# A three-stack transformer kernel whose first norm is applied after its first two products, and whose modulation slabs are spread later over the opening

## What is computed

```python
h = rmsnorm(x, norm_mix)                      # x * rsqrt(mean(x*x) + eps) * gain
proj = h @ w_in                               # qa, ka, va, ra, a_lr, qb, kb, vb, gates
log_a = log_sigmoid(a_lr @ w_lr_up + b_forget) / TAU
...
mod_lat = silu(c) @ ada_w[i] + ada_b[i]       # modulation rows, needed only by the second stack
```

## Time and profile before

| | us |
|---|---|
| median of 3 runs | 1387.56 (1385.98 to 1390.21) |
| the profiled execution | 1386.29, of which its span 1384.5 |
| PE busy in the span | 1356.4 |
| opening: m2's first product / m24's first product | 28.81 / 212.01 |
| longest wait of PE | 7.6, at the start |

### The profile page before, as it was taken

One profiled execution on the slowest core, in us unless ns is written; L12 is line 12 of the kernel. 1 busy time (PEld: TensorE's weight loads), 2 busy tenths in 40 slices (PEclk: granted clock), 3 DMA queues, 4 the chain that ended last, 5 costly groups with the idle time before them and its releaser, 6 DMA issues.

```text
span 1384.5 us, 25206 instructions
## 1 busy us (share of the span) xinstructions
PE 1356.4 (98%) x10086; PEld 1236.2 (89%) x10086; DVE 1017.7 (74%) x1330; ACT 856.9 (62%) x1250; POOL 395.4 (29%) x194
## 2 busy tenths in 40 slices
PE   7999999999999999999999999999999999999997
PEld 5788889999999999899999999999998868888886
DVE  3312774858799998788999999776677696665556
ACT  3632565647888866567988575655554486655554
POOL 2442434233100011221100101655562201143332
PEclk9999999999999999999999999999999999999999
DMA  8776775465344444674444547665654613455551
GB/s 323 269 264 237 268 255 204 152 212 187 132 183 170 156 191 182 248 282 159 156 164 178 213 148 263 228 215 216 216 189 182 263 45 135 183 183 182 182 185 58
DMA packets 39574, 272.04 MB, mean 196 GB/s; under 512 B 4612, under 2 KB 5892, under 8 KB 6974
## 3 DMA queue, kind: packets, MB, share of 16 engines
q1 hardware_dynamic: 39486, 270.81, 53.5%
HBM read 269.73 MB, written 1.06 MB: 196 GB/s over the span
## 4 chain that ended last, share of the span: by engine, by line
PE 85%; DVE 7%; DMA 3%; ACT 2%; issue 1%; SPq 0%; POOL 0%; DVEq 0%; ACTq 0%
PE ps L2118 17%; PE ps L2119 16%; PE ps L2120 16%; PE ps L2153 10%; PE ps L766 9%; PE ps L2155 5%; DMA raw<-w_dram 3%; PE ps L2276 2%; PE ps L2167 2%; DVE wlo L1459 2%; PE ps L2177 1%; PE ps L2643 1%; ACT whi L958 1%; PE ps L2629 1%; DVE gates L1637 1%
## 5 line engine op out<-in xcount | busy, mean ns | idle before, releaser
L916 POOL TENSOR_TENSOR wlo<-raw,whi 128x64 fp32r<-128x64 f32 (+1 forms) x185 | 393.1, 2127 | 968.8 <-ACT whi L958 968.4
L1459 DVE TENSOR_TENSOR wlo<-raw,whi 128x1984 fp32r<-128x1984 f32 (+1 forms) x185 | 340.3, 1841 | 245.4 <-ACT whi L958 245.2
L958 ACT ACTIVATE whi<-raw 128x2048 fp32r<-128x2048 f32 x185 | 352.6, 1910 | 248.0 <-DMA raw<-w_dram 136.6
L2118 PE MATMUL ps<-h_both,whi 128*128 128x256 f32 x944 | 272.7, 289 | 0.5 <-ACT gates L1115 0.5
L2119 PE MATMUL ps<-h_both,whi 128*128 128x256 f32 x944 | 267.0, 283 | 0.0
L2120 PE MATMUL ps<-h_both,wlo 128*128 128x256 f32 x944 | 266.9, 283 | 0.0
L2118 PE MATMUL ps<-g_both,whi 128*128 128x256 f32 x752 | 217.0, 289 | 0.0
L2119 PE MATMUL ps<-g_both,whi 128*128 128x256 f32 x752 | 212.7, 283 | 0.0
L2120 PE MATMUL ps<-g_both,wlo 128*128 128x256 f32 x752 | 212.6, 283 | 0.0
L2118 PEld LDWEIGHTS ps<-h_both,whi 128*128 128x128 f32 x944 | 180.8, 192 | 8.3 <-issue 5.1
L2119 PEld LDWEIGHTS ps<-h_both,whi 128*128 128x128 f32 x944 | 180.9, 192 | 0.5
(11 more groups left out here) (327 smaller groups left out, 2508.5 us busy)
## 6 DMA issues: line engine op xcount, KB each, us to landing
raw<-w_dram SPq DMA_DIRECT2D x243, 1024.0 KB, 4.9
sra<-w_dram SPq DMA_DIRECT2D x2, 1024.0 KB, 6.2
mqk<-w_dram SPq DMA_DIRECT2D x2, 1024.0 KB, 6.5
brev<-w_dram SPq DMA_DIRECT2D x2, 1024.0 KB, 7.5
gates<-w_dram SPq DMA_DIRECT2D x2, 1024.0 KB, 8.6
xlat<-xT_dram SPq DMA_DIRECT2D x2, 512.0 KB, 4.8
brev<-w_first_keys_dram SPq DMA_DIRECT2D x1, 1024.0 KB, 9.3
brev<-bias_rows SPq DMA_DIRECT2D x1, 1024.0 KB, 8.6
```

Source lines behind the costliest of these rows:

```text
L916: pool.tensor_tensor(wlo[:, g.slot, part], raw[:, g.slot, part], whi[:, g.slot, part].bitcast(F32), ALU.subtract).then_inc(lo2_done, 1)
L958: act.activation(whi[:, g.slot, :], raw[:, g.slot, :], ACT.Copy).then_inc(hi_done, 1)
L1459: dve.tensor_tensor(wlo[:, g.slot, part], raw[:, g.slot, part], whi[:, g.slot, part].bitcast(F32), ALU.subtract)\
L2118: pe.matmul(out, w[0], x[0], start=start, stop=False, skip_group_check=True)
```

## The change

1. `LEAD` begins a0 m2 a1 m3 a2 m4, that is, an ada slab stands ahead of each mix slab up to m19 (a17), and then two stand ahead of each of m20, m21, m22. The stream is m2 a0 m3 a1 m4 ... m19 a17 a18 m20 a19 a20 m21 a21 a22 m22 a23 m23 m24 m25 m26. After m19 a mix slab is three places behind the one before it, until m23.
2. DVE multiplies the raw input by the gain into `y_raw` (8 products of 128x256), and PE runs the low-rank product and the first key product on it, without waiting for the norm. DVE multiplies both results by the factor per token (`by_token`); it also makes the normed input itself in four 128x512 products instead of eight of 128x256. The low-rank product is laid out in four groups of 32 columns, and `w_lr_up` is stored with 128 rows (256 KB), the bias in row 0.
3. The first key weights are loaded ahead of every slab; m2 and a0 come next, then the small tensors, then m3.
4. Twelve products of `ones` by itself (128x128, into an unused bank) stand at PE's beginning.
5. ACT splits m2 before the normed input and m3 after it; DVE writes 1984 columns of m2's lower part and POOL 64. m2 runs its upper halves first and its lower halves after (`features(..., split=0)`).
6. Banks go by the mix slab's number; the drain of the low-rank result and of the first keys moved from ACT to DVE.

```diff
-ADA_FIRST = 3
-LEAD = [("ada", i) for i in range(ADA_FIRST)]
+LEAD = []
 for _g in range(2, N_MIX):
-    if _g + 1 < N_ADA:
-        LEAD.append(("ada", _g + 1))
+    _now = _g - 2 if _g < 20 else min(2 * _g - 22, N_ADA)
+    LEAD += [("ada", i) for i in range(_now, min(_now + (1 if _g < 20 else 2), N_ADA))]
     LEAD.append(("mix", _g))
...
-def mix_bank(n):
-    return (n + 2) % 4
+def mix_bank(g):
+    return (2 + 2 * g) % 4 if g < 23 else g % 4
...
-                    run(c, name, first, 0, 1)
                     sp.dma_start(first_keys, io["w_first_keys"]).then_inc(s_keys, 16)
+                    run(c, name, first, 0, 2)
...
-                    sp.dma_start(wlr[0:RANK, :], io["w_lr_up"]).then_inc(s_small, 16)
-                    sp.dma_start(wlr[RANK:RANK + 1, :], io["b_forget"]).then_inc(s_small, 16)
-                    run(c, name, first, 1, RING)
+                    sp.dma_start(wlr, io["w_lr_up"]).then_inc(s_small, 16)
+                    run(c, name, first, 2, RING)
...
             root(0)
+            hi(Slab(0))
             split_hi(0, bufA, h_hi)
-            act.wait_ge(lr_done, 1)
-            act.activation(alr[0:RANK, :], ps[0:RANK, 6, 0:T], ACT.Copy).then_inc(mix_drained, 1)
+            hi(Slab(2))
...
+            scale_raw(0)
+            fold_half(0)
+            fold_half(1)
+            scale_raw(1)
+            dve.wait_ge(std_done, 1)
+            order.mark(dve.reciprocal(rstd[:, 1, :], rstd[:, 0, :]))
+            dve.wait_ge(dve_order, order.value())
+            dve.wait_ge(raw_scaled, KT)
+            for t in range(0, KT, 2):
+                by_token(bufA[:, t * T:t * T + 2 * T], y_raw[:, t * T:t * T + 2 * T], 2).then_inc(y_done, 2)
+            dve.wait_ge(lr_done, 1)
+            order.mark(by_token(alr, ps[:, 6, 0:T], 1))
+            dve.wait_ge(dve_order, order.value())
+            dve.memset(alr[0:1, :], 1.0).then_inc(lr_sb, 1)
+            lo(Slab(0))
+            split_lo(0, bufA, H)
+            dve.wait_ge(keys_done, 1)
+            by_token(flat(ka[:, 0:2, :]), ps[:, 0, :], 2).then_inc(keys_sb, 1)
+            lo(Slab(2))
...
+            pe.wait_ge(s_lr, 16)
+            low_rank(0)
+            square_sums(0)
+            pe.wait_ge(s_keys, 16)
+            unsplit_keys(0, 0)
+            square_sums(1).then_inc(ms_done, 1)
+            low_rank(4).then_inc(lr_done, 1)
+            unsplit_keys(0, 1)
+            for k in range(1, KT):
+                for m in range(2):
+                    ins = unsplit_keys(k, m)
```

More of the change, by code:

```diff
@@ L87, in lead_stream @@
 def lead_stream():
-    out, rest = LEAD[:ADA_FIRST], LEAD[ADA_FIRST:]
+    out, rest = [], list(LEAD)
     while rest:
[L91 to L95, removed]
+        n = next(i for i, item in enumerate(rest) if item[0] == "mix")
+        turn, rest = rest[:n + 1], rest[n + 1:]
+        if n:
+            turn.insert(n - 1, turn.pop())
+        out += turn
     return out
@@ L210, in pool_words @@
 def pool_words(use, i=0):
-    if use in BETWEEN or use in ("ffn_lat", "ffn2") and i < 2:
+    if use in BETWEEN or use == "lead" and i == 0 or use in ("ffn_lat", "ffn2") and i < 2:
         return 64
@@ L850, in _ @@
                     sp.dma_start(io["scratch"], flat(state[0:H_MOBA, 0, 0:2, :])).then_inc(tab_out, 16)
-                    run(c, name, first, 4 * RING, 9 * RING + 2)
+                    run(c, name, first, 4 * RING, 8 * RING + 2)
                     sp.wait_ge(tab_out, 16)
@@ L855, in _ @@
                       .then_inc(brev_in, 16)
-                    run(c, name, first, 9 * RING + 2, count)
+                    run(c, name, first, 8 * RING + 2, count)
                     sp.wait_ge(sub_done, 3)
@@ L1151, in _ @@
                         act.wait_ge(tab_done, 1)
[L1152 removed]
+                    drain(g, sra[:, 2 * (g - 15):2 * (g - 15) + 2, :], ACT.Silu)
                 else:
@@ L1687, in _, with scale_raw, fold_half @@
             dve.memset(relb[BUCKETS:BUCKETS + 1, :], NEG).then_inc(s_relb, 1)
-            for i in range(2):
+            dve.wait_ge(s_first, 16)
+            def scale_raw(i):
+                dve.wait_ge(s_x[i], 16)
+                for t in range(4 * i, 4 * i + 4):
+                    dve.tensor_scalar(y_raw[:, t * T:t * T + T], xlat[:, t, :], col("norm_mix", t), None, ALU.mult).then_inc(raw_scaled, 1)
+            def fold_half(i):
                 dve.wait_ge(sq_done, 2 * i + 2)
@@ L2302, in _, with low_rank, square_sums @@
             H, G = (h_hi, h_lo), (g_hi, g_lo)
-            pe.wait_ge(s_memset, 3)
-            for i in range(2):
+            pe.wait_ge(s_memset, 2)
+            for _ in range(WARMING):
+                pe.matmul(ps[:, 7, 0:P], ones[:, :], ones[:, :], start=True, stop=True)
+            def low_rank(k0):
+                pe.wait_ge(raw_scaled, k0 + 4)
+                for k in range(k0, k0 + 4):
+                    r = QUAD * (k % 4)
+                    ins = pe.matmul(ps[r:r + QUAD, 6, 0:T], lr_down[:, k, :], y_raw[:, k * T:k * T + T], start=(k < 4), stop=(k >= 4),
+                                    skip_group_check=True)
+                return ins
+            def square_sums(i):
                 pe.wait_ge(halves_folded, i + 1)
@@ L2479, in _ @@
             for i in range(4):
-                last = max(n for n in range(len(LEAD)) if mix_bank(n) == i)
-                pe.wait_ge(mix_drained, LEAD[last][1] + 1)
+                pe.wait_ge(mix_drained, drained(max(g for g in range(2, N_MIX) if mix_bank(g) == i)))
                 features(Slab(BASE["gla"] + i), i, G)
```

95 lines of the change are left out of this document (44 added, 51 removed).

## The result

Eight runs of the changed kernel took 1391.8 to 1398.0 us, median 1394.3; eight of the kernel before, beside them, 1384.5 to 1390.5, median 1388.4. The ratio of the two is 1.0054, with a 95% interval of 1.0041 to 1.0067: the change makes the kernel slower by half a per cent. The forecast was 1392.0, range 1387.5 to 1396.0; it was added to a median of 1387.6 for the kernel before, so it stood for 4.4 us more, where 5.9 were measured.

The account below looks back on a forecast made before the run. PE, busy 1356.4 of 1384.5 us, was taken as the bound, its waits in the opening deciding: -5.2 (start) - 0.35 (turn) + 9.9 (end) = +4.4 on 1387.6, so 1392.0 us, range 1387.5 to 1396.0.

Parts of the forecast that it names:

- The start: Opening up to m2: m2's first product at 20.7 instead of 28.8 us; less three deferred ada slabs, a 5.2 us gain.
- the floor that was covered: Start: the norm and m2's lower part are done at 19.2 us, 1.5 us before PE reaches m2 at 20.7.
- Rival 5: Start gains less: keys land at 12 us all the same, 3.3 us of gain remain; +6.3, 1393.9 us; chance 0.05.
- The middle: m3 to m18: nothing gained, today's waits come back; the 0.35 us came from a modulation turn falling into an existing wait.
- The end: m20 to m24: waits of 11.7 us in all, less a 1.8 us wait that goes; a net loss of 9.9 us.
- the handover in a shared slot: m20 to m22: split and product come one after the other, 5.55 us from a mix slab's end to the next one's start.
- The wait for probabilities that should vanish: End of the opening: today's second wait for probabilities, 1.8 us, goes, since that round has the whole of m21's delay.
- the tail is milder: End: the last two waits, 3.5 us ahead of m23 and m24, vanish; +0.9, 1388.5 us; chance 0.22.
- faster: End: `hi` of m20, m21, m22 costs PE nothing, only the start counts; -7.3, 1380.3 us; chance 0.06.
- loads land late: End: loads take 6.65 instead of 4.85 us, m21 starts 0.8 later and m23 1.8; +7.0, 1394.6 us; chance 0.12.
- rival 4: Clock falls in the new idle stretches of 3.2 and 3.55 us, 1.6 us lost twice; +7.6, 1395.2 us; chance 0.08.
- main case: Whole kernel: start, middle and end as summed, +4.4 us, 1392.0 us, own range 1390 to 1394; chance 0.47.

Follow-up runs that it names:

- e5: Changed kernel with deferred ada slabs handed back later and slots alternating, without the twelve `ones` products: 1384.2 us, against 1380.4 with them.
- e7: Changed kernel with ada slabs handed back later, low rank and first keys reading the normed input behind both sums: 1385.8 us, against 1380.4 without that edit.
- e6: Changed kernel with ada slabs handed back later, first keys loaded behind m2's slab: 1385.6 us, against 1380.4 without that edit.
- e1: Changed kernel with only the tail of the loading order changed so slots alternate from m20 on, PE's order untouched: 1384.0 us.
- e4: Changed kernel with lower parts of m20 to m24 split 1984 columns on DVE and 64 on POOL: 1389.8 us.
- e8: Changed kernel with ada slabs handed back later, first round's exponentials and normalising ahead of m19's split: 1378.6 us, 0.9928 of the kernel before.
- e11: Changed kernel with only the first round's exponentials and normalising moved ahead of m19's split: 1390.9 us.
- e3: Changed kernel with unread `ones` products in PE's idle time before m20, m21, m22 and the first transposes of probabilities: 1390.7 us.
- e9: e8 measured again, in another session: 1378.5 us, 0.9942 of the kernel before.
- e10: e8 without the twelve `ones` products: 1384.2 us, against 1378.5 for e9 on the same chip.
- e12: Kernel before, with only the twelve `ones` products put ahead of its first work: 1385.3 us, ratio 0.9989.

## Why the prediction was right, and where not

**The start.** Forecast and trace agree step by step: keys' first product 10.1, measured 10.03; m2 20.7, measured 20.71; m2's lower part, the floor that was covered, 19.2, measured 19.39; z's end 7.9 us after m2's start, measured 7.7; clock full from 7.6 us on, yes by the pace of the sums (1.13 us a pair, where e5 has 2.08). The gain of 8.1 us at m2 less three ada slabs is what it should be. e7 shows that it needs the input taken ahead of its norm, e6 that the keys' landing sets it. Rival 5, that the start gains less, did not come true.

**The middle.** Forecast 0.35 us; measured about 2. m18's first product came at 163.84 us before and comes at 153.34 now, 10.5 earlier, with three ada slabs and a turn (3.4) fewer ahead of it: 7.1, of which the start explains 5.1. m7's wait fell from 1.2 to 0.6 us, one of 0.5 ahead of m9 and the 0.4 ahead of the means went, 1.5 us in all; the rest is small differences that were not followed up. The step "each wait of today in that stretch comes back" was wrong for these three, in the kernel's favour.

**The end.** The term that decided is the handover in a shared slot, 5.55 us each. Forecast of PE's idle time ahead of m20 to m24: 3.2, 3.55, 1.4, 1.7, 1.85, in all 11.7; measured 3.40, 3.41, 1.82, 1.43, 1.68, in all 11.74. m24's wait has the cause that was given: DVE took the row maximum of round 2 behind m23's lower part. Its rows in the changed kernel:

```profile
209.47 1.23 DVE L1461 TENSOR_TENSOR wlo<-raw,whi 128x1024 fp32r<-128x1024 f32 x1 [6.53 <-ACT whi L963]
210.61 1.23 DVE L1742 TENSOR_TENSOR ps<-ps,brev 128x1024 f32<-128x1024 f32 x1
...
218.09 6.75 DVE L1461 TENSOR_TENSOR wlo<-raw,whi 128x1024 fp32r<-128x1024 f32 x2
```

e1 removed the shared slots and the waits went; e4 shortened the pieces and they shrank. The wait for probabilities that should vanish vanished. So the rivals "the tail is milder" and "faster" are out, and so is "loads land late": no `hi` of m20, m21 or m22 was released by a load, and m23's, which waited for its own, began 8.0 us after m21's end, where 8.1 had been forecast.

**What was missed.** Two terms. The wait ahead of the first transposes grew from 1.44 us to 2.59, since ACT does m19's `hi`, which waits for its load, ahead of the exponentials; e8 and e11 took it away. And the clock: three times after 160 us it was at half. Against the same pieces at full pace (mix slab 6.01 us from its first product's start to its last one's end, transposes to m19 3.03, both in e8) m20 took 7.47, m21 8.38 and the stretch from the transposes to m19 4.67: 1.5 + 2.4 + 1.6, with 0.3 in a20 and a21 (2.27 us instead of 1.93) 5.8 us in all. This was rival 4, at 0.08, and by the prediction's own sign (PEclk under 1.00 after 160 us) it holds; but its chance stood beside that of the main case, as if only one of the two could come true, and it came on top. Its price was two falls at 1.6 us each; the trace has three, of 1.6, 1.5 and 2.7. The sum of the trace: -5.1 - 2.0 + 1.15 + 11.75 - 1.8 + 5.8 = +9.8 us, measured 9.6: m24 came at 221.6, where 216.4 had been forecast. By the medians the loss is 5.9 us and e3 puts the clock's share at 3.6 or more. That this is less than 5.8 fits with other executions losing less there and with those of the kernel before losing some as well (their mean clock is 0.992 to 0.999 in e1's session), but no second trace of either kernel shows it.

The Trainium skill ("TensorE: Matmul & The Clock Gate", HAM oscillation) says that idle gaps between matmuls bring the throttled clock back; the change is a case of it, with e3 as its test: the same waits with PE kept busy left the clock at 1.00 from 160 to 200 us. The page has this follow from a gap that is long enough; here the length did not decide alone, and the measurement holds: the clock fell after 1.45 us of waiting in e3, after 1.8 and 2.0 in e11 and after 2.3 in e4, and did not fall after 2.4 in e4 and after 3.4 in e11.

So the forecast of 1392.0 had the right mechanism at the right price, and two errors of opposite sign beside it, 1.65 us too little gained in the middle and 6.95 too little lost at the end. In the trace they leave 5 us. That the median of 1394.3 lies within the range, 0.3 above the main case's own 1390 to 1394, is in part luck: the middle's gain covers some of the clock's loss, and the median execution took 2.9 us less than the profiled one.

## What to carry to other kernels

When two orders meet (the order of work and a ring of buffers), look at the distance between successive users of the same kind modulo the ring: an extra item between them can put them into one slot, and a split that overlapped the product then stands in line with it. The remedy may be a list of entries in the order of loading, with the work untouched. And where a change makes an engine wait that has two clocks, add the price of the clock to that of the wait: the two come together.

## What had not been expected of the hardware

- PE's clock fell behind waits of 1.45 to 3.8 us, and behind others of 2.4 (e4) and 3.4 us (e11) it did not. It differs between executions of one kernel: e1 ran at a mean clock of 0.999 in 1381.3 us and at 0.994 in 1386.2. Keys that came 2.4 us later made m2 4.0 us later (e6); with the norm first m2 came 6.1 us later, where the order alone had been priced at 3.9 (e7).
- How steady a kernel's time is doesn't tell whether its clock holds. e8 and e9 repeat within 1.5 us at a mean clock of 0.998 or 0.999, and e11 repeats within 1.4 us at 0.993 to 0.996, with waits of up to 3.4 us and two falls in its trace. e5, whose trace has no wait of PE above 1.4 us after its first product and no fall in the opening, spreads over 6.5 us; the kernel before spreads over 6 to 11. What makes the difference no run here shows.
- Twelve products without a reader, 5 us in otherwise idle time, are worth 3.8 and 5.7 us in the median (e5, e10), though the traces of single executions show 0.56 and 0.6 us at the start; in a start with waits behind them (e12) m2 came no earlier.
